# Turning a finished block's h in 32x32 blocks on VectorE instead of transposing it on TensorE

## The reference

```
proj = rms_norm(h, norm_mix_w) . w_in            # u | z | xBC | dt, 4632 columns
h   += concat(pool_mixer(u), ssd_mixer(z, xBC, dt)) . w_out
hn   = rms_norm(h, norm_ffn_w)                   # h * rsqrt(mean(h*h) + eps) * norm_ffn_w
h   += square(relu(hn . w_ff1)) . w_ff2          # 4096 hidden columns
out  = rms_norm(h, norm_f_w)                     # meta positions dropped
```

## Time and profile before

| what | value |
|---|---|
| time, median of 3 runs | 2672.59 us |
| the profiled execution, span | 2674.7 us (2.1 us more than the median) |
| instructions | 37670 |
| mean granted TensorE clock | 0.999 |
| DMA | 531.14 MB in 224451 packets, 14074 of them under 512 B |

### The profile page before, as it was taken

The page is one execution under the profiler, slowest core; times in us unless marked ns, Lnnn a source line. Parts: engine busy times, 40 slices in busy tenths (PEclk is TensorE's granted clock), DMA queues, the critical chain, the costliest instruction groups (busy, mean ns, idle before and its releaser), DMA issues.

```text
span 2674.7 us, 37670 instructions
## 1 busy us (share of the span) xinstructions
PE 2654.5 (99%) x14058; PEld 2225.0 (83%) x14058; DVE 1636.3 (61%) x2204; ACT 1281.4 (48%) x2562; POOL 1091.7 (41%) x866
## 2 busy tenths in 40 slices
PE   8999999999999999999999999999999999999998
PEld 6788778888888888898888888888888888888887
DVE  6788714788136883367853576574445766666667
ACT  4577654666245672355734454555454322222223
POOL 2133440335003441023444688665554535353434
PEclk9999999999999999999999999999999999999999
DMA  9977676654646546555574555774445842423324
GB/s 327 299 255 244 237 247 223 251 181 172 220 174 245 194 160 236 190 215 181 188 267 142 200 197 203 259 259 154 152 151 207 309 145 96 164 103 126 118 95 157
DMA packets 224451, 531.14 MB, mean 199 GB/s; under 512 B 14074, under 2 KB 97022, under 8 KB 214798
## 3 DMA queue, kind: packets, MB, share of 16 engines
q1 hardware_dynamic: 224270, 528.74, 55.3%
HBM read 382.74 MB, written 145.95 MB: 198 GB/s over the span
## 4 chain that ended last, share of the span: by engine, by line
PE 95%; DMA 2%; SPq 1%; DVE 1%; issue 0%; POOL 0%; ACT 0%; POOLq 0%; ACTq 0%
PE bank L2257 23%; PE bank L2225 22%; PE bank L1832 21%; PE bank L1939 12%; PE bank L1919 7%; PE bank L2023 2%; PE bank L1985 1%; PE bank L2040 1%; PE bank L2003 1%; PE bank L2011 1%; DMA w_scr<-w_both 1%; DMA meta_w<-in_w_in 1%; PE bank L1991 1%; PE bank L1958 1%; DMA raw<-in_w_out 0%
## 5 line engine op out<-in xcount | busy, mean ns | idle before, releaser
L1832 PE MATMUL bank<-hnT_hi,w_ring 128*128 128x512 f32 x1152 | 369.4, 392 | 0.0
L2257 PE MATMUL bank<-w_first,T_hi 128*128 128x512 f32 x896 | 275.8, 389 | 0.0
L2387 DVE SCALAR_TENSOR_TENSOR acc<-pre,par,acc 128x512 f32<-128x512 f32 x240 | 211.6, 882 | 90.4 <-ACT pre L1345 84.6
L1832 PEld LDWEIGHTS bank<-hnT_hi,w_ring 128*128 128x128 f32 x1152 | 216.3, 188 | 44.5 <-ACT win_tmp L1474 0.5
L2742 DVE TENSOR_TENSOR acc_th<-bank,acc_th 128x512 f32<-128x512 f32 x224 | 150.0, 686 | 155.4 <-PE bank L2257 154.0
L2225 PE MATMUL bank<-T_hi,w_both 128*128 128x512 f32 x768 | 242.4, 389 | 0.5 <-DVE ff L2683 0.5
L1939 PE MATMUL bank<-w_ring,T_hi 128*128 128x512 f32 x768 | 239.0, 392 | 0.1
L1832 PE MATMUL bank<-hnT_lo,w_ring 128*128 128x512 f32 x576 | 224.5, 390 | 0.0
L2257 PEld LDWEIGHTS bank<-w_first,T_hi 128*128 128x128 f32 x896 | 168.2, 188 | 34.9
L1919 PE MATMUL bank<-w_ring,hnT_hi 128*128 128x384 f32 x768 | 196.0, 336 | 0.0
L1832 PE MATMUL bank<-hnT_hi,w_both 128*128 128x512 f32 x544 | 183.1, 408 | 2.3 <-ACT pre L1345 2.3
(11 more groups left out here) (315 smaller groups left out, 6315.2 us busy)
## 6 DMA issues: line engine op xcount, KB each, us to landing
w_ring<-w_scr SPq DMA_DIRECT2D x312, 512.0 KB, 4.3
T_scr<-stage SPq DMA_DIRECT2D x32, 1792.0 KB, 6.7
w_scr<-w_both SPq DMA_DIRECT2D x100, 512.0 KB, 4.3
pair_raw<-in_w_ff SPq DMA_DIRECT2D x36, 1024.0 KB, 5.6
third<-T_scr SPq DMA_DIRECT2D x28, 1024.0 KB, 4.9
pair_raw<-T_scr SPq DMA_DIRECT2D x28, 1024.0 KB, 4.9
sums<-sums_scr SPq DMA_DIRECT2D x64, 384.0 KB, 5.0
raw<-in_w_in SPq DMA_DIRECT2D x36, 512.0 KB, 6.4
```

Of the source, the lines that this page charges most:

```text
L1832: mm = nc.tensor.matmul(bank[s][:, :], w[:, k, :], t[:, k, :], start=(k == 0 and j == 0), stop=(k == KT - 1 and j == 2))
L2257: mm = nc.tensor.matmul(bank[4 * half + t][:, :], a[:, k, tok], w[:, k, :], start=(SECOND[q % 7] not in GOES_ON and k == 0 and j == 0), st ...
L2387: ins = nc.vector.scalar_tensor_tensor(acc[:, s, 0:TB], pre[:, s, k:k + TB], w, acc[:, s, 0:TB], ALU.mult, ALU.add)
```

## The change

The multiplication by the inverse root and by norm_ffn_w is one VectorE instruction per tile, with norm_ffn_w broadcast over the partitions (`ffn_w`, a new tile loaded at the start). A second VectorE instruction turns the tile in 32x32 blocks: within each quarter of 32 partitions, each block of 32 features changes places with the 32 tokens. What is then still missing, that blocks of features go to other partitions, is done by the store's addresses: four DMAs per tile, each with runs of 32 tokens (128 B) in DRAM. `hT_scr` is laid out by feature tile, [KT, P, TB], so that one pattern covers a feature's place. TensorE's transposes, ScalarE's scalings and copies of blocks 0 to 2 are gone. The four tiles are turned in VectorE's steps 5 to 8; the stores go out behind the loads and sums of units 11, 12, 13 and 14. ScalarE waits for the last tile before it writes c_both, and y_high for all 16 stores.

```diff
-        hT = at("hT", [P, KT, TB], T_hi_at + 4 * 2048)
+        ffn_w = sb("ffn_w", [P, D_MODEL])
+        h_turn = at("h_turn", [P, CH, D_MODEL], T_hi_at + 4 * 2048)
-        hT_scr = nc.dram_tensor("hT_scr", [BLOCKS, P, KT, TB], F32).ap()
+        hT_scr = nc.dram_tensor("hT_scr", [BLOCKS, KT, P, TB], F32).ap()
 ...
@@ SyncE
+                sp.dma_start(ffn_w[:, :], norm_ffn_w[0].partition_broadcast(P)
+                             ).then_inc(late_consts, 16)
+                def store_turned_h(b, t):
+                    h_turned.wait(sp, b, t + 1)
+                    features = hT_scr[b].rearrange("k (j a) n -> a (k j) n", a=32)
+                    for s in range(4):
+                        tok = t * P + 32 * s
+                        sp.dma_start(features[:, :, tok:tok + 32],
+                                     h_turn[32 * s:32 * s + 32, t, :].rearrange(
+                                         "p (c f) -> p c f", f=32)).then_inc(hT_stored.sem, 16)
-                        if n == 11 and b:
-                            hT_ready.wait(sp, b - 1, KT)
-                            sp.dma_start(hT_scr[b - 1], hT[:, :, :]).then_inc(hT_stored.sem, 16)
+                        if b and 11 <= n < 15:
+                            store_turned_h(b - 1, n - 11)
@@ ScalarE
                     if b and q == 0:
-                        hT_stored.wait(act, b - 1, 16)
+                        hT_stored.wait(act, b - 1, 64 * CH)
-                        for t in range(CH):
-                            h_scale(b - 1, t)
-                        if b and 1 <= n < 5:
-                            for k in (2 * n - 2, 2 * n - 1):
-                                h_tile(b - 1, k, hT[:, k, :], bank[2 + k % 2][:, :])
+                            if q == 0:
+                                h_turned.wait(act, b - 1, CH)
@@ TensorE
-                        if b and 1 <= n < 5:
-                            for k in (2 * n - 2, 2 * n - 1):
-                                ...
-                                h_transposes(b - 1, k, bank[2 + k % 2])
@@ VectorE
+                def h_turning(b, t):
+                    h_rstd.wait(dve, b, 1)
+                    h_stored.wait(dve, b, 16 * CH)
+                    steps.link(nc.vector.scalar_tensor_tensor(h[:, t, :], h[:, t, :], r2[:, t:t + 1],
+                                                              ffn_w[:, :], ALU.mult, ALU.mult))
+                    nc.vector.transpose(h_turn[:, t, :], h[:, t, :]).then_inc(h_turned.sem, 1)
                         if n:
                             finish(b, n - 1)
+                        if b and n >= 5:
+                            h_turning(b - 1, n - 5)
```

More of the change, by code:

```diff
@@ L337, in build @@
         h_rstd = sig("h_rstd", 1, 0)
[L338 to L341, removed]
+        h_turned = sig("h_turned_then_scaled", CH, 0)
+        h_scaled = h_turned
+        hT_ps = sig("hT_ps", 0, 0)
+        hT_ready = sig("hT_ready", 0, 0)
+        hT_stored = sig("hT_stored", 64 * CH, 0)
         dtT_ps = sig("dtT_ps", 1)
@@ L606, in hT_quarter @@
             k = 4 * (int(name[0]) - 1)
-            return hT_scr[2 * half + int(name[1]) - 1, :, k:k + 4, :]
+            return hT_scr[2 * half + int(name[1]) - 1, k:k + 4].rearrange("k p t -> p k t")
         def w2_quarter(c, name):
@@ L864, in _ @@
                                 state_ready.wait(sp, b, STEPS)
-                                hT_stored.wait(sp, 1, 16)
+                                hT_stored.wait(sp, 1, 64 * CH)
                                 for k in range(4):
@@ L971, in _ @@
                         hT_ready.wait(sp, LAST, KT)
-                        sp.dma_start(hT_scr[LAST, :, 0:5, :], hT_last[0][:, :, :]
+                        sp.dma_start(hT_scr[LAST, 0:5].rearrange("k p t -> p k t"), hT_last[0][:, :, :]
                                      ).then_inc(hT_stored.sem, 16)
-                        sp.dma_start(hT_scr[LAST, :, 5:KT, :], hT_last[1][:, :, :]
+                        sp.dma_start(hT_scr[LAST, 5:KT].rearrange("k p t -> p k t"), hT_last[1][:, :, :]
                                      ).then_inc(hT_stored.sem, 16)
@@ L1072, in _ @@
                     low_part(pool, N)
-                pool.wait_ge(late_consts, 16 * 5)
+                pool.wait_ge(late_consts, 16 * 6)
                 steps = Steps(pool, pool_sem)
@@ L2089, in _ @@
                             nv_ready.wait(pe, b, 1)
-                            pe.wait_ge(late_consts, 16 * 5)
+                            pe.wait_ge(late_consts, 16 * 6)
                             for i in range(4):
@@ L2099, in _ @@
                                 meta_products(m)
-                        if b and 1 <= n < 5:
-                            for k in (2 * n - 2, 2 * n - 1):
[L2103 to L2108, removed]
-                                h_transposes(b - 1, k, bank[2 + k % 2])
                         if n == (5 if b else 6):
-                            if b:
-                                hT_ready.wait(pe, b - 1, KT - 1)
                             running_totals(b)
@@ L2117, in _ @@
                             acs_ready.wait(pe, b, 1)
-                            if b:
-                                hT_ready.wait(pe, b - 1, KT)
-                            else:
+                            if b == 0:
                                 pe.wait_ge(c_act, PW_SCALED)
@@ L2750, in final_scale @@
                     dve.wait_ge(f_rstd, n + 1)
-                    dve.wait_ge(late_consts, 16 * 6)
+                    dve.wait_ge(late_consts, 16 * 7)
                     nc.vector.scalar_tensor_tensor(
```

## The result

The changed kernel takes 2710.42 us (median of 4 runs, 2710.05 to 2710.76) where the one before took 2672.74 beside it: a ratio of 1.0136 over their runs (95% interval 1.0122 to 1.015). Its profiled execution has a span of 2709.0 us, 34.3 more than before, and ends 1.4 us short of the median.

What follows compares the result with a forecast made beforehand. TensorE, 99% busy, was taken as the bound. Per block -3.5 + 1.0 + 9.4 + 1.6 = +8.5, three blocks +25.5, opening +1.2: +26.7 on the 2674.7 us span, or 2700 as median; range 2664 to 2752.

Steps and rivals of the forecast that it cites:

- Removed: TensorE's transposes of h in blocks 1 to 3: four pieces of 0.87 us off the chain, 3.5 us per block.
- The totals' wait: TensorE waits 1.0 us per block for running-total copies queued behind the first tile's turning on VectorE (bounds 0.4 and 2.5).
- The stall at the z weights: Small-packet stores ahead in the DMA queue delay the group's last z weights; TensorE stalls 9.4 us per block.
- The clock: After standing still at the z weights, TensorE runs at a lower granted clock: 1.6 us more per block.
- The opening: Broadcasting norm_ffn_w adds 512 KB to the full queue at the kernel's start: 1.2 us (bounds 0 and 1.2).
- Their issue costs SyncE some 16 x 0.4 = 7 us: Issuing the 16 stores per block takes SyncE some 7 us, costing nothing because it otherwise waits for units there.
- rival A: The queue takes h's store by its bytes, or loads pass it: no z-weight stall, 2666.3 us; chance 0.17.
- landings of the last stores over 15 us: Sign that the forecast is right: h's last stores in each block take over 15 us to land.
- C: Packets of h's store cost 7 to 10 ns, the stall spending the transposes' gain: 2667 to 2678 us; chance 0.10.
- B: A small store packet costs what a 512 B one does, 29 ns, or more: stall 23.0 us, 2740 us; chance 0.23.
- The forecast's 15.7 ns: Queue price of each 128 B packet of h's store, from a line through two rows of loads: 16.1 us per block.
- The prediction's formula: Stall at the z weights: 1,024 packets per engine times price, less the old store's 4.8 us and 1.9 us slack.

Runs made afterwards that it cites:

- e2_copies_first: Changed kernel with the copies of the running totals put ahead of the multiply and turning of h on VectorE: 2703.47 us, 1.0112 of the kernel before.
- e9_one_run_copies_first: e3_one_run (output likewise not the reference's) with the copies of the running totals ahead of the turning: 2666.75 us, 0.9975 of the kernel before.
- e1_runs: Changed kernel, same 16 DMAs, with runs of 128, 256 and 512 B in blocks 1, 2 and 3 (output not the reference's): 2683.41 us, one run.
- e3_one_run: Changed kernel with h's store as one DMA of 16 KB runs per block (output not the reference's): 2669.69 us, 0.9981 of the kernel before.
- e7_behind_z: e2_copies_first with all 16 stores behind the load of the group's last z weights: 2687.47 us, 1.0053 of the kernel before.
- e6_long_runs: Changed kernel, copies first, turned tiles side by side: 512 B runs, 4 DMAs a block, h's loads and output stores undoing the token order: 2687.64 us, 1.0049.
- e11_four_dmas: e8_spread_long with each tile's store to h_scr, and the output likewise, as four DMAs of 32 partitions: 2668.42 us, 0.9981 of the kernel before.
- e4_early: Changed kernel with two of the four tiles' stores issued early, the others behind units 11 and 12: 2685.35 us, 1.0046 of the kernel before.
- e5_act_queue: Changed kernel with the same 16 stores issued by ScalarE on its own queue instead of SyncE: 2716.75 us, 1.016 of the kernel before.
- e8_spread_long: e6_long_runs with one store behind each of units 11 to 14, and h_scr and output stored reordered by one DMA per tile: 2744.16 us, 1.0262.

## Why the prediction was right

Forecast 2700, measured 2710.4, inside its own case (packets of 11 to 22 ns) and on its side. By its own steps, per block:

- **Removed**, -3.5: as forecast. No other wait took the transposes' place.
- **The totals' wait**, +1.0: 1.3 (4.0 in three). A turning took 1.25 us where 1.24 was taken, and its multiply 1.28. e2_copies_first and e9_one_run_copies_first show that this was avoidable.
- **The stall at the z weights**, +9.4: 11.4 (34.2 in three). This term is most of what the forecast lacks, 6 us of 7.6 on the span. The place, the three times and the releaser were right. e1_runs shows that it goes with the packets' size, e3_one_run that nothing else makes it, e7_behind_z that it needs the store to stand ahead of the load (0.6 us is left of it there).
- **The clock**, +1.6: 1.8 in block 1, where the granted clock was 0.71 on the mean of that z piece.
- **The opening**, +1.2: 0.2. TensorE came out of that gap 1.5 us later (81.20 against 79.69), but its next unit took 5.70 us against 7.11: its granted clock there was 1.00 against 0.76, and it had the time back.

**The step that failed** is "Their issue costs SyncE some 16 x 0.4 = 7 us [...] nothing, as long as the queue itself stays behind". The issues took 27.5 us in block 1 (9.66 + 5.72 + 6.24 + 5.86), and the chain passes through them. The price came out nearly right all the same, since what holds SyncE grows with the packets (e1_runs), which the text priced in the queue. But two signs that it named read wrong. It said that z weights landing within 8 us of their issue would mean rival A: the weight loads of 470 to 500 us landed 5.2 to 8.5 us after theirs (median 5.9), the last z weights after 6.4, and the kernel was slower, since the issue itself was 11 us late. And it looked for landings of the last stores over 15 us: the longest was 11.1. Both count from the issue, and the queue's delay had gone in front of it. The right sign is the time at which the load is issued.

Of the rivals, A and C fell with the stall itself and with the packets' records: 13.4 ns is not near the 4.7 of its bytes, and lies above C's 7 to 10. Against C's 8.4 us for the whole store stand 1,024 x 13.4 ns = 13.7 us. B, at 29 ns and more, fell by the same record. A rule that it leaned on, of the Trainium skill ("DMA: Bandwidth & Descriptors", Specifications), asks for 512 B and speaks of a read-modify-write below. In the records of e1_runs 128 B costs 13.4 ns and 512 B 27.2, close to a straight line of 8.8 ns and 0.036 per byte: no step shows at 512 B, only a fixed cost that small packets do not spread. The forecast's 15.7 ns was near that, from rows of loads.

What is left is a size. The prediction's formula (packets x price, less 4.8 and 1.9) with the recorded prices gives 512 x 18.1 ns = 9.3, so 2.6 us of stall for 256 B, and 256 x 27.2 ns = 7.0, so 0.3 for 512 B: as e1_runs measured (2.6 and none). For 128 B it gives 13.7, so 7.0, where 10.8 to 11.4 were measured. The trace's packet records tell where the missing 4 us are. From the start of the group's first unit to the landing of the last z weights, on the mean of the three blocks, the 128 B packets take 13.7 us of the sixteen engines' time, as priced. But the 4 KB packets of the weights take 22.2 us where they took 18.9 before (194 ns each against 168), and the engines' gaps are 3.0 us against 2.2. In e1_runs the weights' packets have 195, 192 and 165 ns beside stores of 128, 256 and 512 B. So the loads are slower beside small packets, which the formula leaves out; how that comes about no run shows. That it fits at 256 B is in part a coincidence, since the gaps there (0.3 us) make up for the slower weights. It was luck in part, then, that the forecast came as near as it did: its 15.7 ns, 2.3 too many, put 2.4 us into the store's price that belong to the weights'.

## What to carry to other kernels

When data movement is handed from TensorE to a store's addresses, count the runs, not the bytes: a fourfold longer run took the stall from 11 us to none, and a layout that lengthens the run (turned tiles side by side) kept most of a gain that 128 B runs spent several times over. Put a store of many packets in single DMAs between loads and not as a block ahead of one (four DMAs together left 7.7 us of waits for weights, e6_long_runs; spread out, 3.1, e11_four_dmas), and look at what the issuing engine does next, whichever it is. Look at the dimension with which a DMA's addresses begin: a leading 4 in h's and the output's stores cost 75.7 us against a leading 32.

## What the hardware showed unexpectedly

- A DMA of 1,024 packets can hold the engine that issues it: four took 2.6 us with little else in the queue (e4_early) and 5.7 to 9.7 beside loads, single ones up to 5.92 on SyncE and 7.89 on ScalarE (e5_act_queue). Sixteen in a row, behind one unit's weight load, took 16.6 us, 1.03 each (e7_behind_z).
- 4 KB packets of weights took 194 ns on the mean beside stores of 128 B, where in the same stretch before they took 168; beside stores of 512 B it was 165 (e1_runs).
- A store whose leading dimension is 4 kept a share of 0.24 to 0.26 and moved 49 to 105 GB/s, where one over 128 partitions had 0.84 to 0.95 (e8_spread_long).
- Loads of h in DMAs of 32 partitions landed in up to 23.1 us against 15.3 (e6_long_runs), while stores of 128 KB from 32 partitions took 2.4 us (e11_four_dmas).
- VectorE turns 128x1024 float32 in 32x32 blocks in 1.25 us, the time of a two-input operation of that size and not the 0.75 of the earlier trace rows's fastest.
- After a stand of 12 us TensorE worked at 1.2 GHz for the first part of its next piece, which took 1.8 us more than its 4.17.
